# Reading the page numbers of the second phase one or two issues ahead on SyncE's queue

## The reference

```
k_past = cache_k[l][page_table].reshape(n_seq, n_pages * PAGE_SIZE, N_ATT_HEADS, 2 * ATT_HEAD_DIM)
v_past = cache_v[l][page_table].reshape(n_seq, n_pages * PAGE_SIZE, N_ATT_HEADS, 2 * ATT_HEAD_DIM)
s = jnp.einsum('bqhcd,bkhcd->bhcqk', qi.astype(F32), kf) * scale
p = jax.nn.softmax(jnp.where(mask, s, -jnp.inf), axis=-1)
a = p[:, :, 0] - lam * p[:, :, 1]
return jnp.einsum('bhqk,bkhv->bqhv', a, vf)
```

## Time and profile before

| | |
|---|---|
| median of 3 runs | 2188.78 us (2186.29 to 2192.76) |
| the profiled execution | 2183.23 us, span 2181.6 us |
| granted clock of TensorE, mean | 0.954 |
| busy: PE / DVE / ACT / POOL | 90% / 74% / 24% / 10% of the span |
| moved | 356.66 MB, mean 163 GB/s |

### The profile page before, as it was taken

The page is one execution under the profiler, slowest core; times in us unless marked ns, Lnnn a source line. Parts: engine busy times, 40 slices in busy tenths (PEclk is TensorE's granted clock), DMA queues, the critical chain, the costliest instruction groups (busy, mean ns, idle before and its releaser), DMA issues.

```text
span 2181.6 us, 33591 instructions
## 1 busy us (share of the span) xinstructions
PE 1956.3 (90%) x10618; PEld 1221.0 (56%) x10618; DVE 1612.2 (74%) x3464; ACT 513.7 (24%) x1274; POOL 229.0 (10%) x443
## 2 busy tenths in 40 slices
PE   7899899987998898896869999899989999899887
PEld 4445455544444445453547776676657776676543
DVE  3688777776787777777576887788778877788853
ACT  2233333332433244343201111111101111111110
POOL 1000121111111111111210000000000000000020
PEclk9999999999999899997889999999999999999978
DMA  6354466534434334454444554555545554555564
GB/s 232 115 166 158 160 198 199 189 116 161 153 126 150 117 111 145 165 206 155 151 152 157 171 169 151 175 182 175 170 149 179 180 168 134 175 186 173 170 229 123
DMA packets 165766, 356.66 MB, mean 163 GB/s; under 512 B 21040, under 2 KB 25920, under 8 KB 165600
## 3 DMA queue, kind: packets, MB, share of 16 engines
q1 hardware_dynamic: 131536, 240.41, 33.9%
q0 software_dynamic: 34064, 114.19, 15.9%
HBM read 322.52 MB, written 32.00 MB: 163 GB/s over the span
## 4 chain that ended last, share of the span: by engine, by line
PE 27%; DVE 13%; SPq 5%; DMA 4%; issue 3%; POOL 1%; ACT 0%; DVEq 0%; ACTq 0%
PE PS L777 9%; PE PS L758 5%; DVE sc L1442 3%; PE PD L513 3%; DVE Kt L1437 3%; SPq L2173 3%; PE PS L873 2%; SPq L2180 2%; DMA Kt<-in_cache_k_dram 2%; DMA Vt<-in_cache_v_dram 2%; DVE Pr L2297 1%; PE PS L939 1%; PE PO L955 1%; PE PS L1015 1%; PE PO L956 1%
## 5 line engine op out<-in xcount | busy, mean ns | idle before, releaser
L412 PE MATMUL PT<-W,xT 128*128 128x512 f32 x960 | 440.1, 607 | 1.2 <-ACT xT L1075 1.1
L1437 DVE TENSOR_TENSOR Kt<-Kt,qb 128x1024 f32<-128x1024 f32 x256 | 312.2, 1219 | 48.5 <-DMA Kt<-in_cache_k_dram 42.0
L1442 DVE TENSOR_REDUCE sc<-Kt 128x16 f32<-128x1024 f32 x256 | 312.1, 1219 | 8.0
L412 PEld LDWEIGHTS PT<-W,xT 128*128 128x128 f32 x960 | 180.6, 196 | 197.0 <-issue 195.0
L873 PE MATMUL PS<-region 128*128 128x512 f32 x512 | 236.6, 606 | 5.5 <-ACT Pr L1330 5.0
L1112 ACT ACTIVATE Pr<-PS,negm 128x512 f32<-128x512 f32 (+7 forms) x192 | 165.3, 864 | 176.1 <-DVE negm L1456 158.9
L481 PE MATMUL PO<-region,PTs 128*128 128x128 f32 x1088 | 150.7, 290 | 27.5 <-issue 26.7
L513 PE MATMUL PD<-Vt,pst 128*8 128x512 f32 x912 | 126.6, 627 | 49.6 <-DMA Vt<-in_cache_v_dram 49.6
L481 PEld LDWEIGHTS PO<-region,PTs 128*128 128x128 f32 x1088 | 139.6, 203 | 46.3 <-issue 34.1
L457 PE MATMUL PS<-region,Q 64*128 64x512 f32 (+3 forms) x640 | 151.4, 585 | 11.3 <-ACT Pr L1112 11.3
L1458 DVE TENSOR_REDUCE negm<-PS 128x1 f32<-128x640 f32 (+3 forms) x64 | 65.3, 1021 | 121.3 <-PE PS L457 121.3
(11 more groups left out here) (382 smaller groups left out, 2650.7 us busy)
## 6 DMA issues: line engine op xcount, KB each, us to landing
Kt<-in_cache_k_dram SPq DMA_DIRECT2D x512, 256.0 KB, 3.4
Vt<-in_cache_v_dram SPq DMA_DIRECT2D x264, 256.0 KB, 3.5
Vt<-in_cache_v_dram POOLq DMA_DIRECT2D x192, 256.0 KB, 4.1
W<-in_w_in_dram SPq DMA_DIRECT2D x4, 2048.0 KB, 18.7
xT_scratch<-xT POOLq DMA_DIRECT2D x16, 512.0 KB, 6.4
W<-in_w_in_dram POOLq DMA_DIRECT2D x4, 2048.0 KB, 10.5
region<-in_x_prompt_dram POOLq DMA_DIRECT2D x16, 448.0 KB, 4.2
out_dram<-region POOLq DMA_DIRECT2D x16, 448.0 KB, 3.4
```

What stands on the lines that cost most here:

```text
L412: mm = pe.matmul(Pj, xT[:, c, :], W[:, b, c, :], start=(c == 0), stop=(c == DC - 1))
L1437: link(ve.tensor_tensor(kp, kp, qb[:, :].unsqueeze(1).to_broadcast([P, 2, G]), ALU.mult))
L1442: ve.tensor_reduce(sc[:, g % 2, bass.ds(r16, 2), :].rearrange("p a c -> p (a c)"), kp.rearrange("p a (c d) -> p (a c) d", d=64), X, ALU.ad ...
```

## The change

The list `ORDER_A` is written out as a function, `late_slots`, with the same order of pages. The order of the buffers' waits and of the transfers stays; the four reads of page numbers of a tile move: the second eight key numbers from ahead of K4 to ahead of K2, the second eight value numbers from ahead of V4 to ahead of K4, the next tile's key numbers from ahead of its K0 to ahead of K6, and the next tile's value numbers from ahead of its V0 to between the load of the input and V6. The last tile reads none for a next one; the first tile's are both read ahead of its K0.

```diff
-ORDER_A = "K0 V0 V1 K1 K2 V2 V3 K3 K4 V4 V5 K5 K6 V6 V7 K7".split()
...
+            def key_pair(it, s, pair):
+                page_pair(kc, Kt[:, s % 2], pair, k_load[s % 2], k_used, after(8 * it + (s - 1), TWO_FREE))
+
+            def value_pairs(it, s, four):
+                for half in range(2):
+                    page_pair(vc, Vt[:, half], four[2 * half:2 * half + 2], v_load[half], v_used, after(4 * (it - 4) + s // 2, ONE_ON))
+
+            def late_slots(t, keys, values):
+
+                it = t + NT
+                key_pair(it, 0, keys[0:2])
+                value_pairs(it, 0, values[0:4])
+                key_pair(it, 1, keys[2:4])
+                more_keys = page_numbers(16 * it + 8, 8)
+                key_pair(it, 2, keys[4:6])
+                value_pairs(it, 2, values[4:8])
+                key_pair(it, 3, keys[6:8])
+                more_values = page_numbers(16 * (it - 4) + 8, 8)
+                key_pair(it, 4, more_keys[0:2])
+                value_pairs(it, 4, more_values[0:4])
+                key_pair(it, 5, more_keys[2:4])
+                keys = page_numbers(16 * (it + 1), 8) if t + 1 < NT else None
+                key_pair(it, 6, more_keys[4:6])
+                if t + 2 <= NT:
+                    turned_x(t + 2)
+                values = page_numbers(16 * (it - 3), 8) if t + 1 < NT else None
+                value_pairs(it, 6, more_values[4:8])
+                key_pair(it, 7, more_keys[6:8])
+                return keys, values
...
+            keys, values = page_numbers(16 * NT, 8), page_numbers(16 * (NT - 4), 8)
             for t in range(NT):
-                slots(t + NT, ORDER_A, lambda: turned_x(t + 2) if t + 2 <= NT else None, 13)
+                keys, values = late_slots(t, keys, values)
```

More of the change, by code:

```diff
@@ L30 @@
 READ = 4
-ORDER_A = "K0 V0 V1 K1 K2 V2 V3 K3 K4 V4 V5 K5 K6 V6 V7 K7".split()
-ORDER_OPEN = "K0 V0 V1 K1 K2 K3 K4 V2 V3 K5 K6 V4 V5 K7 V6 V7".split()
 ORDER_K = [f"K{s}" for s in range(SLOTS)]
@@ L2188, in slots @@
                     u = 2 * (s % READ)
[L2189 to L2196, removed]
+                    if s % READ == 0:
+                        keys = page_numbers(16 * it + 2 * s, 2 * READ)
+                    page_pair(kc, Kt[:, s % 2], keys[u:u + 2], k_load[s % 2], k_used, after(8 * it + (s - 1), TWO_FREE))
+            def key_pair(it, s, pair):
[24 more added lines that the diff above has]
+                return keys, values
             load_tail(sp, xbuf, ax_in)
```

## The result

The changed kernel takes 2196.64 us (median of 20 runs, 2183.56 to 2205.45), the kernel before 2186.65 us (20 runs, 2178.96 to 2196.57): ratio 1.0045, 95% interval 1.0031 to 1.0059. It is 10 us slower; the forecast was 13 us faster.

What follows compares the result with a forecast made beforehand. PE and DVE, waiting for pages issued behind SyncE's number reads, bound the kernel. Regular tiles +2, tiles 4, 8 and 12 −12, tile 0 −1.6, tile 15 −1.8: −13.4 us from 2188.8, so 2175 us, range 2158 to 2185.

Steps and rivals of the forecast that it cites:

- both stalls of V4/V5 and K5: PE's 1.05 us wait for V4/V5 and DVE's 2.46 us for K5, both to go; at most 1.8 us a tile.
- F: The end of K3's sums on DVE in each tile, from which the prediction counts times; 1244.35 us in tile 2.
- rival A: Full gain: V6/V7 not late, at reads of 4.4 us and landing in 4.05; 45 us gained, 2144 us, chance 5%.
- part (3): Next tile's value numbers read ahead of V6: V6 issued 3.4 us later, PE stands 2.2 us, regular tiles lose 0.2 us.
- part (4): Opening tiles 4, 8 and 12 gain 4.0 us each, 12 us together; tile 0 gains 1.6 us.
- B: Length of one read of page numbers ahead of K6 or V6, taken as 4.75 us, bounds 4.4 and 6.6.
- The landing of four pages: V6/V7's time from first issue to all landed, taken as 5.8 us; 4.05 as lower bound, 6.45 in tile 9.
- C: Rival: slower, both new reads meet six pages in flight and take the longest pointer loads; 2210 us, chance 8%.
- A and B: Two rivals: V6/V7 not late (2144 us, chance 5%), or late by 1.2 us less than forecast (2158 us, 12%).
- opening tiles: Tiles 4, 8 and 12, where PE's 4.46 us stall at V4/V5 (tile 4) goes; 4.0 us gained each.
- The signs of being wrong: Reads over 5.5 us between K5 and V6, DVE waiting for K6, or no wait at V6/V7.

Runs made afterwards that it cites:

- the shorter filler: Changed kernel plus three full matmuls on TensorE ahead of the V6/V7 group in tiles 1 to 14: 2183.98 us, ratio 0.9983 to the kernel before.
- the dense filler: Changed kernel plus four full matmuls on TensorE ahead of the V6/V7 group in tiles 1 to 14: 2189.66 us, ratio 1.0037 to the kernel before.

## Why the prediction was wrong

The mechanism was right, place by place: both stalls of V4/V5 and K5 go, V6 is issued at F + 12.4 (forecast 12.3), its group starts at F + 18.3 in tile 2 (18.2), tile 15 needs no late read and has its group at F + 15.9, and with the two late reads taken back the kernel is 42 us under the kernel before, where rival A's sum for "V6/V7 not late" was 45.

**The step that failed** is in part (3): "L948 follows 1.0 us behind and L955 0.5 us behind that". It took what follows a stall of 2.2 us at the durations of the full clock. The rows of before had the warning: part (4) itself notes that the eight matmuls behind a stall of 4.46 us took 1.89 us instead of 1.05, and counts their return to 1.05 as gain, but the new stall was charged nothing of the kind. In the changed kernel the group, the transposes and L953/L954 run at half clock in part of the tiles. It costs in two places. From the group's start to L953 it is up to 1.3 us more (2.73 in tile 1 against 1.46 in tile 5); from L953 to the start of the next projection, over the output's and the state's matmuls, it is up to 1.7 us more (4.31 us in tile 1, up to 4.33 in the second profile, against 2.68). The projection and what follows up to F take the same in a regular tile whether the clock had fallen or not, 35.0 us (35.4 up to F of tile 10). Added up over tiles 1 to 14, against 1.47 and 2.68 us at full clock, this is 12 us in the first profile of the changed kernel and 26 us in the second, 19 in the mean. With the clock held by the shorter filler the kernel stands 4 us under the kernel before instead of 10 above it: **some 14 us of a miss of 23**, give or take 5 by the two intervals. The filler itself puts the group 0.25 us later, 3.5 us in 14 tiles; with these the clock's share is 17 to 18 us, which agrees with the 19 of the traces.

**Two terms of the sum were somewhat too small.** B was 4.75 us for each read; in tile 2 they were 4.4 and 5.2, since the table's load behind K6 and the input took 1.75 us, not 0.90. In the mean of tiles 1 to 14 V6 is issued at F + 12.6, 0.3 us behind the forecast. The landing of four pages was put at 5.8 us; in tile 2 it is 1.55 + 4.2 = 5.8, and in tile 1 V6/V7 came later, their group at F + 19.0; in the mean landing adds between 0.1 and 0.2 us. Together the group is at F + 18.65 instead of F + 18.2, which is 6 us in 14 tiles; with the clock's share this makes up the miss, within the noise.

Of the rivals, C had the right side and the wrong mechanism: it asked for reads of over 5.5 us each, and V6's issue at F + 12.6 leaves 4.9. A and B asked for earlier pages, and these did not come. What the sum said of opening tiles (4.0 us gained) came out at 2.8 in tile 4 for the same reason, the clock behind a stall of 3.19 us. The signs of being wrong that the prediction named (long reads, a wait for K6, no wait at V6/V7) did not include this one; K6 was not waited for, V6/V7 were, and the reads were 4.9 us in the mean. PE's waits ahead of V6/V7 in tiles 0 to 14, put at some 30 us, are 43.8 in the first profile.

The Trainium skill's page "DMA: Bandwidth & Descriptors", section "Anatomy of one DMA — SWDGE (gpsimd) path", has the fit from which the prediction estimated 4.4 us for four pages. This trace does not agree either, with 5.8 us in tile 2; by the fit the forecast would have been 20 us lower and the miss larger.

The best version is the change without its last part: 2141 us with the key numbers ahead of K6 and the value numbers back ahead of V0, or 2143 with both back, each 1.9% under the kernel before; the two do not differ by more than the noise.

## What to carry to other kernels

When a wait in an in-order queue is to hide work, compare the wait that stands in front of each issue with the length of that work, one by one, and add up what is put ahead of the same issue: the reads of a tile's second eight numbers, moved to the waits ahead of K2 and K4, were worth 42 us; the two reads of 4.4 and 5.2 us ahead of V6, where 3 us of wait and 2.7 us of slack were to be had, cost 52 us. A stall on TensorE is priced with its length and with the slower matmuls behind it; where the profile has the same line behind a stall and without one, its two durations are the start of that price, and all matmuls up to the clock's return belong to it (here nearly half of it lay behind L953). If a buffer comes late, asking for it later in the engine's order can give most of what fetching it sooner gives: 39 of 52 us here, from two moved lines.

## What the runs showed of the hardware

The granted clock fell behind stalls of 2.1 to 4.1 us in tiles 1 to 14 of the two profiles of the changed kernel, but not each time: with 3.03 us of wait the eight matmul records took 1.89 us in tile 1 and 1.04 us in tile 3 of one profile, and the second profile of the same kernel took 11 us more for the same phase. With only the value numbers moved the group took 1.82 us behind a stall of 1.48 us in tile 4. A filler of sixteen matmul records of 24 rows and 8 columns (1.90 us) did not keep the clock up in tile 5, where 0.85 us of wait was left; six records of 128 by 128 (2.74 us) did in tile 1, and in tile 10 with 1.56 us of wait left. Why the clock falls in one tile and not in another the runs do not show. The Trainium skill's page "TensorE: Matmul & The Clock Gate", section "HAM oscillation — how this bites in real kernels", describes waits for transfers between short stretches of matmuls that make the clock fall again and again; the trace agrees in kind, with a granted clock of 0.98 and 0.96 over the phase with the change and 1.00 with the dense filler.
